# Attention's modulation pieces: weights times condition on VectorE, the sum over partitions on TensorE, in eight latent-key blocks

## The reference

```python
sc = jax.nn.silu(c)
mx = (sc @ w_ada[l] + b_ada[l]).reshape(B, N_MOD, D)[:, :, None, :]   # (1024) @ (1024, 6144)
u_x = x * (1.0 + mx[:, 1]) + mx[:, 0]
h_x = u_x @ w_in[l]
y_x = mixer_out(h_x, kv_all, ...)            # attention of 6 latent heads and 6 grouped-query heads, conv, w_o
x = layer_norm(ALPHA * x + mx[:, 2] * y_x, ln1_g[l], ln1_b[l])
y_x = sq_relu_mlp(x * (1.0 + mx[:, 4]) + mx[:, 3], w_mlp1[l], w_mlp2[l])
x = layer_norm(ALPHA * x + mx[:, 5] * y_x, ln2_g[l], ln2_b[l])
```

## Time and profile before

| what | us |
|---|---|
| median of 3 runs | 3046.53 (3046.21 to 3046.75) |
| the profiled execution's own time | 3052.03 |
| its span | 3050.2 |
| TensorE busy in the span | 2932.1 (96%) |
| VectorE busy in the span | 2270.0 (74%) |
| GpSimd busy in the span | 1380.3 (45%) |

### The profile page before, as it was taken

One profiled execution on the slowest core, in us unless ns is written; L12 is line 12 of the kernel. 1 busy time (PEld: TensorE's weight loads), 2 busy tenths in 40 slices (PEclk: granted clock), 3 DMA queues, 4 the chain that ended last, 5 costly groups with the idle time before them and its releaser, 6 DMA issues. The chain is left out here.

```text
span 3050.2 us, 43167 instructions
## 1 busy us (share of the span) xinstructions
PE 2932.1 (96%) x15760; PEld 2201.1 (72%) x15760; DVE 2270.0 (74%) x3170; ACT 1327.7 (44%) x1911; POOL 1380.3 (45%) x833
## 2 busy tenths in 40 slices
PE   5999978999999999999999989999999999999997
PEld 3889865566666566666658768887888888887886
DVE  4445456788887888788777788776777667887788
ACT  3222233444444444444443456555555543433452
POOL 1233324677767867686732244332333144214420
PEclk7999989999999999999999989999999999999998
DMA  6232379524354332434147885447444687897883
GB/s 262 60 87 78 101 234 325 120 74 81 98 119 95 78 81 63 85 80 85 30 149 254 285 311 205 155 152 292 152 153 153 221 299 287 288 315 278 301 289 131
DMA packets 252013, 526.65 MB, mean 173 GB/s; under 512 B 35568, under 2 KB 110832, under 8 KB 240624
## 3 DMA queue, kind: packets, MB, share of 16 engines
q1 hardware_dynamic: 243504, 493.55, 50.4%
q10 hardware_dynamic: 8320, 30.61, 2.6%
HBM read 363.19 MB, written 160.76 MB: 172 GB/s over the span
## 5 line engine op out<-in xcount | busy, mean ns | idle before, releaser
L1369 DVE TENSOR_REDUCE h_mpart<-a_mx 128x1 f32<-128x512 f32 x920 | 537.7, 632 | 153.4 <-PE a_mx L1474 140.6
L1298 POOL TENSOR_TENSOR a_acc_p<-a_acc_p,a_pf 128x1024 f32<-128x1024 f32 x237 | 572.6, 2416 | 152.1 <-ACT a_pf L1349 121.5
L1349 ACT ACTIVATE a_pf<-o_y 128x1024 f32<-128x1024 f32 x432 | 441.8, 1026 | 380.0 <-PE o_y L1521 372.6
L2662 POOL TENSOR_TENSOR stream<-raw_rows 128x512 f32<-128x512 f32 x158 | 217.3, 1377 | 374.6 <-DVE f_wx L2474 360.7
L2671 POOL TENSOR_TENSOR f_y<-f_y,raw_rows 128x1024 f32<-128x1024 f32 x72 | 196.5, 2730 | 350.1 <-DMA raw_rows<-in_w 350.1
L2726 PE MATMUL o_y<-slots 128*128 128x512 f32 x1176 | 298.1, 391 | 1.8 <-DVE slots L2481 1.8
L2718 PE MATMUL o_y<-slots,f_wx 128*128 128x512 f32 x1140 | 266.5, 392 | 4.8 <-DMA slots<-s_uc 4.8
L2726 PEld LDWEIGHTS o_y<-slots 128*128 128x128 f32 x1176 | 221.6, 189 | 49.4 <-DVE slots L2481 3.1
L2718 PEld LDWEIGHTS o_y<-slots,f_wx 128*128 128x128 f32 x1140 | 215.7, 189 | 50.3 <-DMA slots<-s_uc 5.2
L573 PE MATMUL p_main<-win_hi,u_hi 128*128 128x512 f32 (+2 forms) x528 | 196.8, 373 | 15.2 <-PEq L75 14.4
L573 PE MATMUL p_main<-win_hi,u_lo 128*128 128x512 f32 (+2 forms) x528 | 195.2, 370 | 0.0
(11 more groups left out here) (343 smaller groups left out, 6136.6 us busy)
## 6 DMA issues: line engine op xcount, KB each, us to landing
s_hx<-o_area SPq DMA_DIRECT2D x224, 256.0 KB, 2.6
raw_rows<-s_hx SPq DMA_DIRECT2D x112, 512.0 KB, 4.4
f_y<-in_w SPq DMA_DIRECT2D x104, 512.0 KB, 5.8
raw_rows<-in_w SPq DMA_DIRECT2D x72, 512.0 KB, 5.9
raw_rows<-in_w SPq DMA_DIRECT2D x32, 1024.0 KB, 4.9
s_uc<-o_area SPq DMA_DIRECT2D x76, 256.0 KB, 5.6
raw_rows<-in_w_ada SPq DMA_DIRECT2D x8, 2048.0 KB, 8.8
low<-s_mix SPq DMA_DIRECT2D x32, 512.0 KB, 5.2
```

The source lines that it names most:

```text
L1298: nc.gpsimd.tensor_tensor(acc[:, :], left[:, :], pf[(b * KT + kt) % NPF][:, :], ALU.add).then_inc(added_p, 1)
L1349: nc.scalar.activation(pf[n % NPF][:, :], sc[n % 2][:, :], ACT.Exp, scale=SCALES[0 if is_mla(b) else 1]).then_inc(exped, 1)
L1369: nc.vector.reduce_max(mpart[b % 2][:, s + 4 * half, k:k + 1], bank(("pair", c), half)[:, 0:CHUNKS[k][1]], AX.X).then_inc(mx_read, 1)
L2662: nc.gpsimd.tensor_tensor(out, w1_part(n, first), w1_part(n, second), plus(sign)).then_inc(sum_set, 1)
```

## The change

The matrix product of a piece is split in another way. VectorE multiplies the weights of each k with that k's condition value (one per partition) and adds over k into `ada_row`: one `tensor_scalar` for k = 0 and seven `scalar_tensor_tensor` for k = 1 to 7 (`weigh`). They are spread over the steps `ADA_STEPS` of the block. TensorE no longer runs `modulations`; in `modulation_columns` it multiplies `ada_row` with ones instead of `g.sel`, which sums over all 128 partitions. The pieces move to the blocks 2, 3, 6, 7, 10, 11, 14 and 15, all latent. The load of the next piece's weights moves ahead of `store` on SyncE's queue.

```diff
-        MOD_BLOCKS = (0, 2, 4, 6, 8, 12, 16, 20)
+        MOD_BLOCKS = (2, 3, 6, 7, 10, 11, 14, 15)
...
-        ADA_BATCH, ADA_COPY, ADA_TURN = 11, 11, 14
+        ADA_STEPS, ADA_TURN = (3, 4, 5, 7, 8, 9, 10, 12), 14
+        ADA_SETS = KD + 1
...
-                if b in MOD_BLOCKS and kt == ADA_BATCH:
-                    banks(("ada", b), (ada_set, 2 * MOD_BLOCKS.index(b) + 1))
...
+                if b - 1 in MOD_BLOCKS[:-1]:
+                    n = MOD_BLOCKS.index(b - 1)
+                    sp.wait_ge(ada_set, ADA_SETS * n + KD)
+                    load_wa(n + 1)
                 if b:
                     store(b - 1)
-                if b - 1 in MOD_BLOCKS[:-1]:
-                    n = MOD_BLOCKS.index(b - 1)
-                    sp.wait_ge(ada_done, 2 * n + 1)
-                    load_wa(n + 1)
...
+            def weigh(i, k):
+                scalar = g.cond[:, 2 * k:2 * k + 1]
+                if k == 0:
+                    dve.wait_ge(wa_in, 16 * (i + 1))
+                    need(dve, ada_done, i)
+                    ins = nc.vector.tensor_scalar(ada_row[:, :], wa[:, k], scalar, None, ALU.mult)
+                else:
+                    dve.wait_ge(ada_set, ADA_SETS * i + k)
+                    ins = nc.vector.scalar_tensor_tensor(out=ada_row[:, :], in0=wa[:, k], scalar=scalar, in1=ada_row[:, :], op0=ALU.mult, op1=ALU.add)
+                ins.then_inc(ada_set, 1)
...
-                    if b in MOD_BLOCKS and kt == ADA_COPY:
-                        dve.wait_ge(ada_done, 2 * i + 1)
-                        nc.vector.tensor_copy(ada_row[:, :], bank(("ada", b))).then_inc(ada_set, 1)
+                    if b in MOD_BLOCKS and kt in ADA_STEPS:
+                        weigh(i, ADA_STEPS.index(kt))
...
-            def modulations(i):
-
-                pe.wait_ge(wa_in, 16 * (i + 1))
-                bank_free(pe, ("ada", MOD_BLOCKS[i]))
-                for k in range(KD):
-                    mm = ada_strip(nc, g, bank(("ada", MOD_BLOCKS[i])), wa, k)
-                mm.then_inc(ada_done, 1)
-
             def modulation_columns(i):
-                pe.wait_ge(ada_set, 2 * i + 1)
+                pe.wait_ge(ada_set, ADA_SETS * i + KD)
...
-                    mm = nc.tensor.matmul(bank(("turn", MOD_BLOCKS[i]))[:, 2 * c:2 * c + 2], ada_row[:, c * P:(c + 1) * P], g.sel[:, :], start=True, stop=True)
+                    mm = nc.tensor.matmul(bank(("turn", MOD_BLOCKS[i]))[:, 2 * c:2 * c + 2], ada_row[:, c * P:(c + 1) * P], g.ones[:, 0:2], start=True, stop=True)
...
-                        if i is not None and kt == ADA_BATCH:
-                            modulations(i)
```

More of the change, by code:

```diff
@@ L1074, in stage_attend @@
                 if b in MOD_BLOCKS and kt == ADA_TURN:
-                    banks(("turn", b), (ada_set, 2 * MOD_BLOCKS.index(b) + 2))
+                    banks(("turn", b), (ada_set, ADA_SETS * (MOD_BLOCKS.index(b) + 1)))
                 if b == W_BLOCK and kt == 0:
@@ L1203, in _ @@
                 if b == NSB - 2:
-                    sp.wait_ge(ada_done, 2 * len(MOD_BLOCKS))
+                    sp.wait_ge(ada_set, ADA_SETS * len(MOD_BLOCKS))
                     for k, row in enumerate(g.rows):
@@ L1440, in _ @@
                         i = MOD_BLOCKS.index(b)
-                    if b in MOD_BLOCKS and kt == ADA_COPY:
-                        dve.wait_ge(ada_done, 2 * i + 1)
-                        nc.vector.tensor_copy(ada_row[:, :], bank(("ada", b))).then_inc(ada_set, 1)
+                    if b in MOD_BLOCKS and kt in ADA_STEPS:
+                        weigh(i, ADA_STEPS.index(kt))
                     if b in MOD_BLOCKS and kt == ADA_TURN:
-                        dve.wait_ge(ada_done, 2 * i + 2)
+                        dve.wait_ge(ada_done, i + 1)
                         m = slice(M0 + i * MT, M0 + (i + 1) * MT)
@@ L1451, in _ @@
             low(NSB - 1)
-            dve.wait_ge(ada_set, 2 * len(MOD_BLOCKS))
+            dve.wait_ge(ada_set, ADA_SETS * len(MOD_BLOCKS))
             nc.vector.tensor_scalar(g.mods[:, 32:40, :], g.mods[:, 32:40, :], 1.0, None, ALU.add).then_inc(ada_set, 1)
@@ L1581, in _ @@
                     if b == W_BLOCK and kt == 0:
-                        pe.wait_ge(ada_set, 4)
+                        pe.wait_ge(ada_set, 2 * ADA_SETS)
                         for half in range(2):
```

## The result

The changed kernel takes 3090.62 us (median of 7 runs, 3080.07 to 3105.17), the kernel before 3046.21 in the same comparison (3044.23 to 3048.53). The ratio is 1.0148, with a 95% interval of 1.0128 to 1.0168: 44 us slower, where 20 were forecast. The profiled execution is the slowest of the seven, 3105.17 us with a span of 3103.4, so its sums stand against 3050.2 and not against the medians.

A forecast was written before the change was run, and what follows sets the result against it. The prediction took TensorE to bound the kernel, with VectorE near behind in attention. Its terms, -16.8 for the removal, +20.0 for odd and +16.4 for even latent blocks, summed to +19.6: 3066 us, range 3036 to 3092.

The forecast's parts named there:

- What is removed: TensorE's eight weight matmuls a piece and a little waiting: 2.1 us a piece, 16.8 in all, 14.9 as low end.
- The load: The next piece's weights, loaded ahead of `store` on SyncE's queue, land 8.8 us after issue, over 15 us available: no cost.
- last thirds: Last scoring stretch of each latent block, with step 12's product: 0.5 us more, 0.3 less in blocks 7 and 15.
- The wait for GpSimd: In attention, VectorE's two-SBUF-input instructions and GpSimd's block each other: one multiply-and-add per addition, every 2.8 us.
- Steps 7 to 10: Second scoring stretch: three intervals of 2.8 us against TensorE's 1.41 (odd blocks, 4.2) or 1.64 (even, 3.5), plus step 11.
- the entry: Start of the second scoring stretch, VectorE late from steps 3 to 5: 0.9 us reach TensorE in odd blocks, 0 in even.
- Entry 0: Even latent blocks, start of second scoring stretch: no loss, since a 1.64 us step leaves VectorE 0.4 beside its pair.
- the ring of banks: Three banks between TensorE and VectorE: take 0.75 us of lateness at an odd block's entry, and once more at the end.
- The signs named ahead: Second scoring stretches 12 to 14 us, multiply-and-adds 1.5 to 2, TensorE waits 30 to 40, grouped-query blocks shorter by 3.
- rival three: Stalls at their upper ends (3105 us), or values stretches behind second scoring stretches at a lower clock (3109); chance 0.13.
- Rival one: In attention the wait for GpSimd is not paid, multiply-and-adds take 0.69 us: sum -5.6 us, 3041; chance 0.17.
- Rival two: VectorE's idle time takes in all the added work, so 16.8 us or a little less is gained: 3031; chance 0.14.

The follow-up runs named there:

- the place alone: The kernel before, TensorE's matmuls kept, with its pieces in the changed kernel's blocks and the next load ahead of the store: 3043.24 us, ratio 0.9994.
- a GpSimd that reads nothing: Changed kernel with GpSimd's additions in the eight piece blocks replaced by fills of the same tile: 3040.56 us, ratio 0.9980 against the kernel before.
- the one-input run: Changed kernel with each piece's seven multiply-and-adds replaced by a maximum over the same weights, one SBUF input: 3039.77 us, ratio 0.9992 against the kernel before.
- the idle spots: Changed kernel with all eight products where GpSimd is nearly idle, two blocks a piece: 3056.13 us, ratio 1.0031; with convolution blocks' products moved again, 3045.45 us, 0.9991.
- the first-third kernel: Changed kernel with only the three products at steps 3, 4 and 5 of each piece: 3051.97 us, ratio 1.0028 against the kernel before.

## Why the prediction was wrong in size and right in kind

**What is removed.** Forecast 16.8 us, and 3.18 a grouped-query block is what the stretches show. Removal less last thirds is 16.8 - 3.4 = 13.4 in the forecast's terms, and 14.1 in the changed kernel's last scoring stretches. This term was right.

**The load.** No wait of VectorE for it shows, and the place alone is worth nothing (0.9994).

**The wait for GpSimd.** The mechanism that the forecast rests on is shown from both sides: one input in place of two, and a GpSimd that reads nothing, each bring the time to before or under it. The rule of the Trainium skill, SBUF — State Buffer, "Who interferes with whom", agrees with three measurements here. A two-input product waits for a reading addition (1.66 us in the median) and not for a fill (0.74). A reduction with its input in SBUF does not wait for the addition (0.68). The `tensor_scalar`, which the page counts among those that can take both ports, waits for the fill too (0.71 and 0.86 us in place of 0.48).

**Steps 7 to 10.** Their pace was right: in block 7 of the changed kernel the four products begin at 866.46, 868.59, 872.06 and 874.84, 2.79 us apart in the mean, for 2.8. Without the entry the forecast is 3.6 for an even block, 5.05 - 0.9 - 0.8 = 3.35 for blocks 7 and 15 and 5.05 - 0.9 = 4.15 for 3 and 11, 29.4 in all. Measured alone it is 32.1: 3.0 to 3.2 in the even blocks, 3.8 in 7 and 15, but 6.1 in 3 and 11. In those two GpSimd has half a piece of the convolution left, and in the changed kernel the product of step 10 takes 2.88 and 2.89 us there. The sum was of the right size, those two blocks were 2 us short each.

**The step that failed** is the entry, "Entry 0" for the even blocks and "0.9 reach TensorE" for the odd ones, 3.6 us in all. Measured alone it is 22.0. I charged the products of steps 3 and 4 with 0.8 us between them and the one of step 5 with half an addition. But the product of step 5 begins when GpSimd has just begun an addition, in block 7 and in five others: 2.69 us, of which 2.1 are waiting. A wait that the order repeats from block to block is not a random one, and its mean of a half is the wrong estimate. With the 1.67 us of step 4 the first reduction of the second third comes 2.83 us into it in block 7 and not 0.47, so VectorE is 2.4 us late, and the late work is reductions, for which TensorE waits. In the even blocks the product of step 4 takes 2.64 besides, and the 0.4 us that a step leaves VectorE do not take that in: 3.0 us reach TensorE in blocks 10 and 14, and 4.6 and 4.35 in 2 and 6, where the clock fell too. The parts named for the odd entry also do not make its end: 837.65 + 0.8 + 1.2 + 0.56 is 840.2 and not 840.6, so by them only 0.5 us would have reached TensorE. And the ring of banks forgave 0.75 twice in an odd block; nothing in the traces shows a second time.

**How the miss adds up.** The sum was +19.6, and the medians differ by 44. The entry makes 18.4 of the difference, steps 7 to 10 make 2.7, and the values stretches at a lower clock, which the sum has at nothing, 4.5; the last thirds are 0.7 better than forecast.

**The signs named ahead.** The multiply-and-adds (1.63 us in the mean), TensorE's waits (39.7 us) and the grouped-query blocks (3.2 each) came as forecast. The second scoring stretches did not: 14.8 to 17.4 us, where 12 to 14 were named. The sum of the waits fell into its range partly by luck, since it is only 39.7 of the 54.4 us by which these stretches grew, against 33 in the forecast. The measured 3091 also lies inside the stated 3036 to 3092, but only in the part that was there for rival three; the forecast's own sum ended at +40.

**Rivals.** Rival one, the product at 0.69 us, is what the one-input run makes: stalls of 0.4 and 1.1 us in place of its 0.9 and 1.5 (it had 1.1 and 1.7 with the last third). Its sum was -5.6 us; the run came out 2.4 us under the kernel before by the ratio, whose interval holds both that sum and zero. Rival two, everything hidden, fell: even the idle spots gave no more than 0.1%, which is not told from zero. Of rival three the clock came true in part: two of the eight values stretches ran at it, the one at 0.65 took 8.17 us for 5.37, and the scoring stretches of four blocks stood at 0.90 or 0.96. I had called it a case of its own. The runs spread over 25 us, the three shortest (3080 to 3083 us) at a mean clock of 0.981 to 0.982 and the two longest (3101 and 3105) at 0.976, where the seven of before spread over 4. That the spread comes from these stretches is argued, not shown: one run of 3091 has 0.982 too, and in the later comparisons the 20 to 25 runs of before spread over 12 to 19 us by themselves.

## What to carry to other kernels

Before work goes from TensorE to a VectorE that is four fifths busy, look at what GpSimd does at each place, and not only at VectorE's own gaps: a product with two inputs in SBUF costs 0.74 us beside an idle GpSimd and up to 2.9 beside one that adds. Where the order of a loop sets who comes first, take the wait from a walk through the trace at that very place, as the whole remaining instruction, and follow lateness past the stretch in which it arises. And a small gain on the bound engine (here 1.9 us a piece) is quickly gone when the helper engine feeds that engine through a ring of three buffers.

## What the runs showed of the hardware

The multiply-and-add of 128x512 with its scalar read from SBUF takes 0.74 us at the least, where the one with a constant took 0.69; that the scalar makes the difference was not tried. A product that has waited ends some 0.55 us after GpSimd's instruction, in block 7 at 864.68 and 864.13. TensorE's granted clock fell in stretches with waits in which TensorE was still busy most of the time: 11.49 of 14.19 us, at 0.88, in block 6 of the first-third kernel, and 9.99 of 15.94, at 0.96, in block 11 of the changed one, with 0.65 in the values stretch behind. It did not fall in all of them: 9.73 of 14.78 us in block 7 stood at 1.00. In the kernels without long waits it stood at 1.00 in all the stretches shown.
